# One 32-column product ahead of each of 40 matmul units in a streaming encoder step

## What is computed

```
for i in range(DEPTH):                       # DEPTH = 2
    if i % 2 == 0:
        mix, c_new, h_new = ssd_mixer(x, ...)       # Mamba-2 scan, width 2048, out by w_out
    else:
        mix, v_rows = chunk_mlp_mixer(x, ...)       # u * (ws @ norm(v)), width 2048, out by w_out
    x = layer_norm(ALPHA * x + mix, ln1_g[i], ln1_b[i])
    x = layer_norm(ALPHA * x + sq_relu_ffn(x, ffn_w1[i], ffn_w2[i]), ln2_g[i], ln2_b[i])
```

## Time and profile before

| | us |
|---|---|
| median of 3 runs (1644.83 to 1645.43) | 1645.16 |
| the profiled execution, its own time | 1645.21 |
| its span, first to last instruction | 1643.5 |
| PE busy | 1624.6 (99%) |
| PE weight loads busy | 1583.7 (96%) |
| VectorE (DVE) busy | 1168.6 (71%) |
| ScalarE (ACT) busy | 693.7 (42%) |
| GpSimd (POOL) busy | 605.8 (37%) |

### The profile page before, as it was taken

One profiled execution on the slowest core, in us unless ns is written; L12 is line 12 of the kernel. 1 busy time (PEld: TensorE's weight loads), 2 busy tenths in 40 slices (PEclk: granted clock), 3 DMA queues, 4 the chain that ended last, 5 costly groups with the idle time before them and its releaser, 6 DMA issues.

```text
span 1643.5 us, 30293 instructions
## 1 busy us (share of the span) xinstructions
PE 1624.6 (99%) x11954; PEld 1583.7 (96%) x11954; DVE 1168.6 (71%) x2120; ACT 693.7 (42%) x1107; POOL 605.8 (37%) x473
## 2 busy tenths in 40 slices
PE   9999999999999999999999999999999999999996
PEld 9999999999999999999999878999999999999996
DVE  7789999999857784756668633875357865848466
ACT  4556555665214744535332511221025635445325
POOL 0000000000454354443556365556553453544472
PEclk9999999999999999999999999999999999999998
DMA  5233333223222222232323322322222222222222
GB/s 199 80 101 104 103 104 100 74 98 103 75 89 78 78 91 91 90 91 82 98 65 96 123 81 85 97 84 65 90 76 80 87 94 77 91 91 90 91 78 71
DMA packets 44482, 149.54 MB, mean 91 GB/s; under 512 B 5057, under 2 KB 10817, under 8 KB 43073
## 3 DMA queue, kind: packets, MB, share of 16 engines
q1 hardware_dynamic: 37888, 129.98, 24.6%
q10 hardware_dynamic: 6464, 17.74, 3.5%
HBM read 142.55 MB, written 5.15 MB: 90 GB/s over the span
## 4 chain that ended last, share of the span: by engine, by line
PE 89%; ACT 4%; DVE 4%; issue 1%; DMA 1%; SPq 0%; ACTq 0%; DVEq 0%
PE ps L787 54%; PE ps L841 16%; PE ps L1127 6%; PE ps L825 2%; PE ps L775 2%; PE ps L773 2%; PE ps L774 2%; PE ps L1028 1%; PE ps L1011 1%; DVE ta_rows L2295 1%; PE ps L1199 1%; PE ps L1005 1%; PE ps L1003 1%; PE ps L1018 1%; DVE ta_rows L2302 1%
## 5 line engine op out<-in xcount | busy, mean ns | idle before, releaser
L669 POOL TENSOR_TENSOR wl<-wraw,wh 128x512 fp32r<-128x512 f32 x208 | 279.1, 1365 | 366.0 <-ACT wh L1241 202.9
L787 PE MATMUL ps<-xh,wh 128*128 128x288 f32 x1888 | 408.1, 297 | 0.5 <-DVE dtt L1796 0.2
L787 PE MATMUL ps<-xh,wl 128*128 128x288 f32 x1888 | 403.9, 295 | 0.0
L787 PE MATMUL ps<-xl,wh 128*128 128x288 f32 x1888 | 403.3, 295 | 0.0
L787 PEld LDWEIGHTS ps<-xh,wh 128*128 128x128 f32 x1888 | 302.4, 188 | 2.6 <-issue 1.6
L787 PEld LDWEIGHTS ps<-xl,wh 128*128 128x128 f32 x1888 | 303.8, 188 | 0.0
L787 PEld LDWEIGHTS ps<-xh,wl 128*128 128x128 f32 x1888 | 303.5, 188 | 0.0
L653 POOL TENSOR_TENSOR tick<-tick 128x1 f32<-128x1 f32 x80 | 26.0, 325 | 602.6 <-DVE wl L1755 424.8
L656 POOL TENSOR_TENSOR wl<-wraw,wh 128x1024 fp32r<-128x1024 f32 x80 | 201.2, 2515 | 6.7
L787 PE MATMUL ps<-h,wh 128*128 128x288 f32 x1088 | 190.5, 297 | 0.0
L787 PEld LDWEIGHTS ps<-h,wh 128*128 128x128 f32 x1088 | 159.8, 189 | 0.7 <-issue 0.7
(11 more groups left out here) (322 smaller groups left out, 3350.3 us busy)
## 6 DMA issues: line engine op xcount, KB each, us to landing
wraw<-wstream SPq DMA_DIRECT2D x240, 512.0 KB, 3.5
acb<-acum_scratch ACTq DMA_DIRECT2D x8, 1152.0 KB, 6.1
out_y<-r SPq DMA_DIRECT2D x8, 288.0 KB, 2.2
xr<-x ACTq DMA_DIRECT2D x4, 288.0 KB, 6.3
xr<-x SPq DMA_DIRECT2D x4, 288.0 KB, 6.4
hs<-ssm_in ACTq DMA_DIRECT2D x8, 128.0 KB, 6.1
out_ssm_s<-hsn ACTq DMA_DIRECT2D x8, 128.0 KB, 6.3
out_ssm_p<-hp ACTq DMA_DIRECT2D x8, 128.0 KB, 1.9
```

The source lines that it names most:

```text
L669: return pool.tensor_tensor(out, of, rounded, ALU.subtract)
L787: last = mm(m.ps[:, 2 * s + h, 0:moving.shape[-1]], part, moving, start=(k, n) == (0, 0), stop=(k, n) == (KT - 1, 2))
```

## The change

A new function `lead_product` issues one matmul of 32 columns into the slot's second bank, with the first stationary tile of the unit's `wh` and the first 32 columns of the second half of the high activations. `inner_unit` is `unit` with this call between the waits and the 48 products. The unit's own products begin with `start=True` in both banks, so nothing of the lead product stays in the result. `run_inner` is `run_few` with `inner_unit`. It takes the place of `run_few` in `last_block`, in `end_block`, for the units of the last group of the scan, for the two units after it, and for the 14 gate units.

```diff
+    def lead_product(s, part, moving):
+
+        mm(m.ps[:, 2 * s + 1, 0:32], part, moving[:, 0:32], start=True, stop=True)
+
+    def inner_unit(u, w, turn, xh, xl, half=half_of):
+
+        s = w % 2
+        pe.wait_ge(S.w_ready, u + 1)
+        wait(pe, m.slot_evac[s], turn)
+        lead_product(s, m.wh[:, w, 0:P], half(xh, 0, 1))
+        for k in range(KT):
+            w_hi, w_lo = m.wh[:, w, k * P:(k + 1) * P], m.wl[:, w, k * P:(k + 1) * P]
+            for n, (part, x) in enumerate(((w_hi, xh), (w_hi, xl), (w_lo, xh))):
+                for h in range(2):
+                    last = mm(m.ps[:, 2 * s + h, 0:HT], part, half(x, k, h),
+                              start=(k, n) == (0, 0), stop=(k, n) == (KT - 1, 2))
+        last.then_inc(S.gemm_done, 1)
+
     def run_few(u0, n, xh, xl, half=half_of):
         for u in range(u0, u0 + n):
             unit(u, u % RING, slot_turn(u), xh, xl, half=half)
+
+    def run_inner(u0, n, xh, xl, half=half_of):
+        for u in range(u0, u0 + n):
+            inner_unit(u, u % RING, slot_turn(u), xh, xl, half=half)
...
     def last_block(n, u0, xh, xl, half=half_of, first=0):
 
-        run_few(u0 + first, 6 - first, xh, xl, half=half)
+        run_inner(u0 + first, 6 - first, xh, xl, half=half)
...
     def end_block(u0, half):
 
-        run_few(u0 + 2, 2, 0, 1, half=half)
+        run_inner(u0 + 2, 2, 0, 1, half=half)
...
             if last:
-                run_few(U_WOUT + j, 1, m.hh[:, 0:8], m.hl[:, 0:8])
+                run_inner(U_WOUT + j, 1, m.hh[:, 0:8], m.hl[:, 0:8])
...
-    run_few(U_WOUT + 6, 2, m.hh[:, 0:8], m.hl[:, 0:8])
+    run_inner(U_WOUT + 6, 2, m.hh[:, 0:8], m.hl[:, 0:8])
...
-    run_few(gate_unit(2), 1, m.hh, m.hl)
+    run_inner(gate_unit(2), 1, m.hh, m.hl)
...
-    run_few(gate_unit(3), 1, m.hh, m.hl)
+    run_inner(gate_unit(3), 1, m.hh, m.hl)
     for k in range(16):
         if 1 < k < 14:
-            run_few(gate_unit(k + 2), 1, m.hh, m.hl)
+            run_inner(gate_unit(k + 2), 1, m.hh, m.hl)
```

## The result

The changed kernel takes 1649.32 us, the median of ten executions, against 1645.07 us before: a ratio of 1.0026, with a 95% interval from 1.0017 to 1.0034. It is slower by 4.25 us. (One of the ten took 9102 us, for a reason that no trace shows; it is left out of the ratio.) The forecast was 1649.3 us.

A forecast was written before the change was run, and what follows sets the result against it. PE was taken as the bound almost everywhere; 40 lead products at 0.11 us (4.4 us) and a rhythm term of -0.3 us gave +4.1 us on 1645.21 us, so 1649.3 us, with a range of 1646.2 to 1650.4 us.

The forecast's parts named there:

- The bound: Whole kernel: PE is the bound almost everywhere, busy 99% of the span; its waits behind 495 us stay at 2.4 us.
- The absorbed case: PE's waits behind 495 us: the 2.4 us there shrink by what arrives late; +1.7 us, 1646.9 us; chance 0.04.
- The price of a lead: At all 40 lead products: each costs one more weight load on PE, 0.11 us, 4.4 us in all.
- The hidden load: At lead products: PE fetches the unit's first load ahead; +0.6 to +2.9 us, 1645.8 to 1648.1 us; chance 0.13.
- Two passes: At lead products: each runs like plain fp32, two products with two loads; +8.5 us, 1653.7 us; chance 0.07.
- The rhythm term: At 22 units not already behind narrow matmuls: products following a lead run faster, -0.015 us a unit, -0.3 us in all.
- A better rhythm: Inner units: a lead brings them from 6.40 to 6.36 us, 40 x -0.04 us; sum +2.8 us, 1648.0 us; chance 0.06.
- the rhythm carried on: About 190 units' worth behind 396 us keep the lead's phase: -7.6 us, sum -3.2 us, 1642.0 us; chance 0.03.

The follow-up runs named there:

- the places done alone: Two kernels, lead products only at the 22 units directly behind 288- or 512-column products, or only at the 18 behind narrow plain-fp32 products: 1647.18 us each.
- the other tile: Against the changed kernel, the lead product takes the last stationary tile of the unit's high weights instead of the first: 1649.33 us.

## Why the prediction was right

**The bound.** PE was taken as the bound everywhere, with waits that would not shrink. They stayed, but for 0.2 us. (The 2.4 us of the earlier trace rows are five waits, not the six of the prediction.) The absorbed case (1646.9 us) is excluded by the places done alone: each cost its full price in the end time.

**The price of a lead, 0.11 us.** This was the step that carried the forecast, and it was right in both kinds of place, by the loads of 0.11 us in the trace after, by the flat price from 32 to 128 columns, and by 0.11 us for a second lead. It was read from products of 64 and 128 columns in plain fp32; rounded products of 32 columns follow the same load. The hidden load (1645.8 to 1648.1 us) fell with the second lead and with the other tile. The same runs decide between the rows and the page TensorE: Matmul & The Clock Gate of the Trainium skill, section Back-to-back issue gap: its 25 ns for narrow products and 81 ns for streams with loads don't hold for fp32 tiles of 128 columns here, which take 0.11 us. The same page of the Trainium skill, section LDWEIGHTS, gives a load of P columns P / 1.2 ns. For 128 columns that is 107 ns, which agrees with the rows. For a tile of 32 columns it would be 27 ns, an estimate by that page, and the trace shows about 0.05 us.

**Two passes.** The trace shows 40 products and 40 loads, not 80; the plain-fp32 lead shows what it would have been.

**The rhythm term, -0.3 us.** Its total was right, and its parts were not. At the 22 joints it is 0.087 - 0.11 = -0.023 us each, -0.5 us. At the other 18, where I took zero, it is 0.12 - 0.11 = +0.01 us, +0.2 us. Together that is again -0.3 us, which is in part luck. Its reason was wrong: I tied it to a load at its floor, and the lead of 288 columns changed the rhythm with no bare load. Read from start to start in the first `last_block`, every fourth product of an inner unit takes 0.140 us against 0.131 before the change. Behind a lead of 32 columns the first three of these slow products are missing and the rest of the unit is as before: that is about the 0.023 us. What makes them slow stays open.

**A better rhythm, and the rhythm carried on.** Net of a lead of 0.11 us, an inner unit at a joint takes 6.375 us, which is over half of the way from 6.40 to the 6.36 us that this rival names. It failed because at the 18 other places nothing came back, and because 22 x -0.023 us is a third of its 40 x -0.04 us. That the units on `xh` owe their rhythm to the same thing is not shown; theirs moved with addresses alone. Nor was anything carried on: eight units on `xh_ext` of the changed kernel take 51.19 us, as before.

**The range.** By the prediction's own figures it leaves out about the lowest sixth of the hidden load (1645.8 to 1646.2 of 1645.8 to 1648.1 us), not the lowest third, and a price of 0.107 us with a rhythm of -0.7 us gives 1648.8 us and not 1648.5. Neither slip touches the forecast.

## What to carry to other kernels

Where PE is the bound, count for a product the larger of its columns and the load of the next tile. In this kernel a narrow rounded product with a whole tile was so paid as about one load (0.087 to 0.12 us), at either kind of place and for 32 columns as for 128; a plain-fp32 one cost two. Find the floor in the trace by reading loads from start to start at the narrowest products there are; halving the columns there and seeing no change names the limit. And when products of one size show two rates, try moving the tensors in SBUF before touching their order, and read the effect stage by stage: here one shift made some units slower and others faster, and the sum hid it.

## What the hardware showed that I had not expected

Where the tensors lie in SBUF, with the program otherwise the same, moves the rate of 288-column products. From start to start a unit of 48 on `xh` takes 6.37 us at 584 numbers from row to row, 6.40 at 580 and 6.45 at 578. One on the inner rows in `h2` takes 6.40 us in all three kernels, and one on `hid_h` in the first layer 6.40, 6.24 and 6.24 us. With 578 the whole shift made 4.1 us of the whole kernel, as much as the 40 products of the change. The units on `hid_h` are the more useful case: four of the 40 units that the change touches got faster by 0.16 us each, more than a lead product costs, without an instruction added or removed. In them the slow product of every four is gone. Which address did it, why the second layer's two units on `hid_h` did not follow, and whether the others can gain as much, stays open. Turning the order of the halves made inner units up to 0.08 us slower, for a reason that also stays open.
